# A fused two-block network on one core: expert weights asked for in smaller parts, slot-weight transposes inside the up product, and the last pair's gather in two parts

## What is computed

```python
x = x + g1 * (concatenate([y_l, fourier_mixer(f_l, w_four)]) @ w_out)
# hier_moe on t = modulate(rmsnorm(x, norm2), sh2, sc2), 256 tokens
grp = top_k(softmax(t @ w_rg + b_rg), 1)          # 1 of 4 groups
j_top = top_k(softmax(logits of that group), 2)   # 2 of its 8 experts
gate = p_top_grp * p_top / sum(p_top)
y[token] += gate * ((silu(xb @ w_eg[e]) * (xb @ w_eu[e])) @ w_ed[e])
out = rmsnorm(x + g2 * y, final_norm)
```

## Time and profile before

| | us |
|---|---|
| median of three runs | 1468.61 |
| lowest and highest | 1464.35, 1469.03 |
| profiled execution | 1465.74 |
| its span in the trace | 1463.9 |
| PE, DVE, ACT busy | 1322.8, 799.7, 611.3 |
| mean rate of the transfers | 262 GB/s |

### The profile page before, as it was taken

One profiled execution on the slowest core, in us unless ns is written; L12 is line 12 of the kernel. 1 busy time (PEld: TensorE's weight loads), 2 busy tenths in 40 slices (PEclk: granted clock), 3 DMA queues, 4 the chain that ended last, 5 costly groups with the idle time before them and its releaser, 6 DMA issues.

```text
span 1463.9 us, 26277 instructions
## 1 busy us (share of the span) xinstructions
PE 1322.8 (90%) x11196; PEld 1126.5 (77%) x11196; DVE 799.7 (55%) x1223; ACT 611.3 (42%) x946; POOL 85.5 (6%) x65
## 2 busy tenths in 40 slices
PE   7999999999999999999999999888977777777877
PEld 7989798999989888999989999678544344434535
DVE  5557847766467577876558896964112112111213
ACT  5553345444456666455446654753211111111112
POOL 2000000000003100221001000410000000000000
PEclk9999999999999999999999999998999999999998
DMA  9655347544574567355453050329999999999995
GB/s 374 228 204 192 116 173 295 193 174 173 192 312 167 206 275 282 136 200 189 173 211 144 32 231 1 159 101 424 423 427 427 427 427 427 427 428 427 427 427 228
DMA packets 29489, 383.47 MB, mean 262 GB/s; under 512 B 3344, under 2 KB 3488, under 8 KB 6208
## 3 DMA queue, kind: packets, MB, share of 16 engines
q1 hardware_dynamic: 28656, 377.71, 64.2%
q0 software_dynamic: 720, 4.10, 0.7%
HBM read 380.75 MB, written 1.05 MB: 261 GB/s over the span
## 4 chain that ended last, share of the span: by engine, by line
PE 57%; DMA 24%; DVE 11%; ACT 6%; issue 2%; SPq 0%; POOL 0%; DVEq 0%; ACTq 0%; POOLq 0%
PE ps L649 56%; DMA ring<-in_experts 24%; DVE w_lo L1880 3%; DVE work L1892 2%; ACT work L1356 1%; ACT w_hi L1356 1%; DVE work L1880 1%; ACT HM L1356 1%; DVE HM L1880 1%; ACT L1356 1%; DVE act L1880 1%; DMA ring<-in_dense 0%; ACT act L1356 0%; DVE work L2151 0%; DVE small L2048 0%
## 5 line engine op out<-in xcount | busy, mean ns | idle before, releaser
L1880 DVE TENSOR_TENSOR w_lo<-ring,w_hi 128x1024 fp32r<-128x1024 f32 x272 | 339.7, 1258 | 213.0 <-ACT w_hi L1356 212.6
L649 PE MATMUL ps<-in_hi,w_hi 128*128 128x256 f32 x1376 | 390.6, 284 | 17.6 <-DVE w_lo L1880 17.2
L649 PE MATMUL ps<-in_hi,w_lo 128*128 128x256 f32 x1376 | 387.1, 281 | 0.0
L649 PE MATMUL ps<-in_lo,w_hi 128*128 128x256 f32 x1376 | 386.8, 281 | 0.0
L1356 ACT ACTIVATE w_hi<-ring 128x1024 fp32r<-128x1024 f32 x272 | 286.1, 1056 | 236.0 <-PE ps L649 230.7
L649 PE MATMUL ps<-ring,work 128*32 128x256 f32 (+3 forms) x2528 | 204.8, 459 | 95.3 <-DMA ring<-in_experts 86.5
L649 PEld LDWEIGHTS ps<-in_hi,w_hi 128*128 128x128 f32 x1376 | 261.4, 190 | 22.7 <-issue 19.3
L649 PEld LDWEIGHTS ps<-in_lo,w_hi 128*128 128x128 f32 x1376 | 261.4, 190 | 0.3
L649 PEld LDWEIGHTS ps<-in_hi,w_lo 128*128 128x128 f32 x1376 | 261.3, 190 | 0.0
L649 PEld LDWEIGHTS ps<-ring,work 128*32 128x32 f32 (+1 forms) x2528 | 85.4, 119 | 196.3 <-issue 112.3
L1892 DVE SCALAR_TENSOR_TENSOR X<-ps,mod,X 128x256 f32<-128x256 f32 x136 | 59.0, 479 | 248.3 <-PE ps L649 248.3
(11 more groups left out here) (270 smaller groups left out, 1894.7 us busy)
## 6 DMA issues: line engine op xcount, KB each, us to landing
ring<-in_experts SPq DMA_DIRECT2D x90, 2048.0 KB, 23.3
ring<-in_dense SPq DMA_DIRECT2D x82, 2048.0 KB, 8.0
ring<-in_dense SPq DMA_DIRECT2D x4, 512.0 KB, 8.3
work<-in_experts SPq DMA_DIRECT2D x1, 2048.0 KB, 11.5
ring<-in_experts SPq DMA_DIRECT2D x4, 512.0 KB, 21.5
spare<-in_experts SPq DMA_DIRECT2D x1, 1536.0 KB, 11.2
cst<-in_ret_cst POOLq DMA_DIRECT2D x1, 1280.0 KB, 13.1
cst<-in_experts SPq DMA_DIRECT2D x1, 1280.0 KB, 5.9
```

The source lines that it names most:

```text
L649: i = pe.matmul(o, l, r, start=start, stop=stop)
L1880: i = dve.tensor_tensor(out=o, in0=x, in1=y, op=op)
```

## The change

Three edits. First, SP asks for the held units in smaller parts. `cst`, `act2`, `work` 0 to 1024 and the first row of held unit 3 (`work` 1024 to 1536) wait only until PE is done with the last tile `y`; held unit 2 waits for the last `y_ready`; `lr2` still waits for `h_ready`, now behind the load of slot 5; the other four rows of unit 3's first part still wait for `y_lo_ready`. So that `cst` is free, the squares of tiles 4 and 5 (`ysq[2]`) go to `lr2`. Second, PE transposes the slot weights within the up product, behind the gather, and DVE reduces them and writes `SGt` before it makes `hs`. Third, in the last pair only four of the gather's eight pieces are made within the up product and the other four behind the transposes of `hs`, and ACT scales all eight behind its copy of `hT`. The pieces now lie at the same columns of the bank whichever is the first (`c * PAIR`), and the first part of the last gather signals nothing.

```diff
-        ysq = [at(9728, 512), at(10240, 512), at(2048, 512, of=flat_cst), at(0, 512, of=flat_sq)]
+        ysq = [at(9728, 512), at(10240, 512), lr2[:, :, :].rearrange("p a b -> p (a b)"), at(0, 512, of=flat_sq)]
...
             hold(1, spare[:, :], 0)
             first_load(0)
-            sp.wait_ge(s["h_ready"], KD)
+            await_full(sp, TILE["y", KX - 1])
             hold(0, flat_cst, 0)
             hold(0, act2[:, :, :].rearrange("p a b -> p (a b)"), 5)
-            hold(0, lr2[:, :, :].rearrange("p a b -> p (a b)"), 7)
+            hold(1, work[:, 0:2 * FE], 6)
+            hold(3, work[:, 2 * FE:3 * FE], 0)
+            sp.wait_ge(s["y_ready"], KX)
             hold(2, work[:, 9728:9728 + UNIT], 0)
             sp.wait_ge(s["chunk_used"], MIX0 + 2)
             first_load(5)
+            sp.wait_ge(s["h_ready"], KD)
+            hold(0, lr2[:, :, :].rearrange("p a b -> p (a b)"), 7)
             sp.wait_ge(s["y_lo_ready"], KX)
-            hold(1, work[:, 0:2 * FE], 6)
-            hold(3, work[:, 2 * FE:7 * FE], 0)
+            hold(3, work[:, 3 * FE:7 * FE], 1)
             sp.wait_ge(s["chunk_used"], MIX0 + FG)
...
-            HELD_PARTS = 3, 2, 1, 2, 2
+            HELD_PARTS = 3, 2, 1, 3, 2
...
-                    o = ps[:, bk, (c - first) * PAIR:(c - first + 1) * PAIR]
+                    o = ps[:, bk, c * PAIR:(c + 1) * PAIR]
                     for tau in range(2):
                         i = mm(o, t_raw[:, tau, c * P:(c + 1) * P], S2[:, tau, :], tau == 0, tau == 1)
-                i.then_inc(s["gath_full"], 1)
+                if first + count == KD or bk != GATHER_BANK:
+                    i.then_inc(s["gath_full"], 1)
...
                             if up and c == 4:
                                 pe.wait_ge(s["eq_ready"], pair + 2)
-                                gather(0, GATHER_BANK)
+                                gather(0, GATHER_BANK, KD // 2 if last else KD)
+                                pe.wait_ge(s["sgb_ready"], pair + 1)
+                                for tau in range(2):
+                                    i = pe.transpose(ps[:, Y_BANK, tau * P:(tau + 1) * P], SGb[:, tau, :], ident[:, :])
+                                i.then_inc(s["sg_full"], 1)
...
-                    pe.wait_ge(s["sgb_ready"], pair + 1)
-                    for tau in range(2):
-                        i = pe.transpose(ps[:, Y_BANK, tau * P:(tau + 1) * P], SGb[:, tau, :], ident[:, :])
-                    i.then_inc(s["sg_full"], 1)
                     pe.wait_ge(s["hs_ready"], pair + 1)
                     for b in range(2):
                         i = pe.transpose(ps[:, 0, b * P:(b + 1) * P], hs[:, b * P:(b + 1) * P], ident[:, :])
                     i.then_inc(s["ht_full"], 1)
+                    if last:
+                        gather(KD // 2, GATHER_BANK, KD // 2)
                     pe.wait_ge(s["ht_ready"], pair + 1)
...
-                    gathered(1 - p % 2, 0, GATHER_BANK, KD, pair + 3)
+                    if not last:
+                        gathered(1 - p % 2, 0, GATHER_BANK, KD, pair + 3)
                     act.wait_ge(s["ht_full"], pair + 1)
                     fn(hT[:, :, :].rearrange("p a b -> p (a b)"), ps[:, 0, 0:T], ACT.Copy, s["ht_ready"])
                     if last:
+                        gathered(1 - p % 2, 0, GATHER_BANK, KD, pair + 3)
                         load_norm_tables()
...
                     select(p + 1)
-                    dve.wait_ge(s["gs_ready"], pair + 1)
-                    dve.wait_ge(s["gu_full"], pair * 2 + 2)
-                    tt(hs, gs, ps[:, 1, 0:T], MUL, s["hs_ready"])
                     dve.wait_ge(s["sg_full"], pair + 1)
                     weighted = ps[:, Y_BANK, 0:T]
                     dve.tensor_reduce(gcol, weighted, AX_X, ADD).then_inc(s["gcol_ready"], 1)
                     ts(SGt[0:PAIR, 0, :], weighted[0:PAIR], 0.0, ALU.is_gt)
                     ts(SGt[PAIR:P, 1, :], weighted[PAIR:P], 0.0, ALU.is_gt, inc=s["sgt_ready"])
+                    dve.wait_ge(s["gs_ready"], pair + 1)
+                    dve.wait_ge(s["gu_full"], pair * 2 + 2)
+                    tt(hs, gs, ps[:, 1, 0:T], MUL, s["hs_ready"])
```

More of the change, by code:

```diff
@@ L1838, in gathered @@
                 for c in range(first, first + count):
-                    fn(xg[:, par, c, :], ps[:, bk, (c - first) * PAIR:(c - first + 1) * PAIR], ACT.Identity, s["xg_ready"],
+                    fn(xg[:, par, c, :], ps[:, bk, c * PAIR:(c + 1) * PAIR], ACT.Identity, s["xg_ready"],
                        scale=coef[:, 2, c:c + 1], bias=mod[:, 3 * KD + c, 0:1])
```

## The result

| | before | changed |
|---|---|---|
| median of nine executions each | 1466.71 us | 1470.67 us |
| lowest and highest | 1464.35, 1471.61 | 1466.5, 1473.55 |
| ratio, with its 95% interval | 1 | 1.0024 (1.0013 to 1.0034) |

The changed kernel is slower by 0.24%, 3.5 us, with an interval of 1.9 to 5.0 us. The forecast was 0.45 us. The profiled execution of the changed kernel has a span of 1468.6 us.

The account below looks back on a forecast made before the run. Expert-weight transfers were taken to bound the kernel from about 978 us, PE's chain its end. Terms -1.5 + 1.95 = +0.45 us, on a mean of 1466.9, gave 1467.4 us; range 1463 to 1471, 8 in 10 for 1461 to 1472.

Parts of the forecast that it names:

- What bounds the kernel: Whole kernel: expert-weight transfers bound everything from about 978 us; after the last landing at 1429.28 the chain is PE's.
- Part 1: Held units asked for 16.3 us earlier; only the backlog at 1023.97 is won: gain 9.1 - 7.6 = 1.5 us.
- The lower bound of 0.7: Earlier requests: least gain, 0.7 us, if what the engines lost around 1026 stays lost.
- Part 2: Slot weights transposed within the up product: gain 0.1 us for each pair, vanishing in PE's waits for units in 15.
- Part 3: Last pair's gather in two parts: ACT's scaling delays the last down product, cost 1.95 us.
- rival C: Tail: PE's clock falls behind the waits before the last down product; up to +10 us, 1472 to 1477; 9%.
- Rival A: Held units: the earlier start counts in full, -16.3 + 1.95, so 1451 us; 5%.
- Rival B: Start of pair 0: if PE's clock comes back early, it starts 6 us sooner, giving 1461 us; 11%.
- Rivals D: Transfers beside the last heads and `mix_out` (962 to 978) slow engines there: +5 us, 1472; 4%.
- E: Last pair: ACT's scaling doesn't hold PE up, -1.5 - 0.1, 1465.3 us; 12%.
- The sum: Whole kernel: -1.5 + 1.95 = +0.45 us on the profiled execution, 1465.74 to 1466.2 us.
- The level of 1467.4: Forecast time of the changed kernel, taking the mean of four times before, 1466.9 us, as the level.

Follow-up runs that it names:

- part 1 alone: Kernel before with only the earlier requests for held units: ratio 1.0003 (0.9993 to 1.0013).
- the late requests: Kernel before with its held requests waiting for six chunks of `mix_out`, the first going out 4.6 us behind `h_ready`: ratio 1.0024, 3.5 us slower.
- the 9 matmuls alone: Kernel before with 9 more matmuls into an unused bank while PE waits for the routing's mask: ratio 0.9994 (0.9985 to 1.0003).
- the split alone: Kernel before with only the last pair's gather in two parts: ratio 1.0029 (1.0016 to 1.0041), 4.3 us slower.
- the wait filled: Changed kernel with 12 more matmuls while PE would wait for ACT's scaling: ratio to before 1.0018 (1.0008 to 1.0028).
- the requests and the 9 matmuls: Kernel before with the earlier held requests and 9 more matmuls in PE's wait for the routing; slot 0 back 4.7 us sooner: ratio 0.9962, 5.6 us faster.

## Why the prediction failed, step by step

- **What bounds the kernel** held: the transfers to 1429, PE behind it. That the kernel before sits near the point where the two requests meet was in the working (a backlog of 1.5 us at 1023.97) and came out in the runs with 4.6 us later and 4.7 us earlier.
- **Part 1**: request times (961.4 forecast, 961.88), both dry stretches and the unmoved request at 1024 were right. The term was not: 1.5 us of backlog to be won, 0 measured (1.0003, and a landing 9.4 us after the request for 7.6). The landing out of an idle queue was taken as 7.6 us from two other places of the trace; at this place it took 9.4, and 9.2 with part 1 alone, as long as with the backlog before (9.1). The lower bound of 0.7 was still too high. The backlog was hardly one: before, the first reused slot was asked for 3.3 us ahead of the last held part's landing (1027.25) and landed 5.8 us behind it. Asked for 8.6 and 8.3 us ahead, with the late requests and with the 9 matmuls alone, it landed 4.9 us behind it. So 0.9 us was lost in that hand-over before, too. Of the kernels with part 1, the best starts the last gate half 404.7 us after that request, before 405.3: 0.6 us is the most that any of them won, and the changed kernel won nothing (405.6).
- **Part 2**: forecast 0.1 us and nothing elsewhere; the trace has 0.17, and 0.9996 (0.9986 to 1.0006) agrees.
- **Part 3**: PE's later start was forecast at 1.95 us and measured at 1.70 (14.88 against 13.18). What failed is that the sum put the matmuls behind the wait at their old time, with only ACT and the landings looked at for slack: the 2.57 us in which PE waits cost another 2.4 us, because the 96 records that follow run at the lower clock. That is rival C, to which I gave 9%, for spells of some 5 us or more, long enough to leave the bounds of no change. The working had counted 15 slow blocks among 22 behind waits of 2 us or more, and had priced one at 1.65 us, but put that price at nothing in the sum. It came in all three profiled kernels with this wait, ended with the block, and cost 2.41. So it was a term of the sum and not a rival: 1.70 + 2.41 = 4.1 us, and the split alone measured 4.3.
- **Rival A** (the start counts in full) fell with the requests alone. **Rival B** (slot 0 comes back sooner) didn't happen in the changed kernel, but its mechanism was right. Brought about with the 9 matmuls, slot 0 came back 4.7 us sooner, where the working had 6, and the kernel was 5.6 us faster than before. **Rivals D** and **E** fell: 1.0003 with part 1 alone, and ACT's scaling did hold PE up.
- **The sum**: -1.5 + 1.95 = 0.45 should have been 0 + 1.7 + 2.4 = 4.1; measured are 3.5 (1.9 to 5.0). The two misses, 1.5 us of gain that wasn't there and 2.4 us of clock that was left out, point the same way; only the wait, 0.25 too long, made up for a little. The level of 1467.4 was 0.7 above the median of before as measured now, the bound of 0.3% was not passed, and 1470.67 lies in the range; the forecast of next to no change did not hold.

## What to carry to other kernels

Before moving work behind the last stage's wait, follow its consumer: here four of eight pieces moved by 3 us took with them the scaling of all eight, which had been hidden and then stood in the chain. A new wait of PE ahead of a row of matmuls may have to be priced twice, the wait and the slower matmuls behind it (here 2.4 us behind 2.57 of wait, and nothing behind 2.25). And where two bounds lie within a us or two of each other, removing one shows nothing: test the second together with it before dropping the first.

## What the runs showed of the hardware

The same transfer of 2048 KB out of an idle queue doesn't always take the same time. Unit 4, asked for between 1002.2 and 1005.7, landed 7.6 to 8.7 us later in the seven kernels with part 1 (7.9 in the changed kernel, 7.6 with part 1 alone). The first reused slot took 9.4 and 9.2 in these two and 8.8 with the wait filled, but 7.9 to 8.3 in the four kernels that had part 1 and the 9 matmuls, though its neighbour was asked for 1.7 us behind it in all of them. The windows of the changed kernel (columns as above) show how such a transfer starts; a packet is counted in the window in which it starts:

```profile
1025.50:1026.00 0.50, 0.50 (x17) 0.27 (x12) 0.00 (x0) 0.38 (x1) 0.00 (x0) 1.00 1.41 262
1026.00:1026.50 0.50, 0.50 (x16) 0.31 (x12) 0.00 (x0) 0.00 (x0) 0.00 (x0) 1.00 0.00 0
1026.50:1027.00 0.50, 0.50 (x16) 0.15 (x8) 0.00 (x0) 0.00 (x0) 0.00 (x0) 1.00 0.77 328
```

The empty window isn't idle. From 1024.4 to 1026.4 the DMA view has 16 packets for 73.4% of 16 engines' time, 1.47 us a packet; from 1027.4 to 1029.4 it has 52 for 102.6%, 0.63 us a packet. So the first packets out of an idle queue were more than twice as slow. The first 2 us in the kernel with the requests and the 9 matmuls look alike (16 packets, 72.0%), and it landed its slot in 8.0 us; what makes 9.4 of 8.0 is open.

PE's granted clock fell within a single wait of 2.57 us, which was for ACT and not for data (1.00 until 1446.5, 0.50 from 1447), and came back with the end of the block. The block behind that wait was slow in three kernels of three, that behind 2.25 us was not (2.84 us), and that behind 1.91 and 2.26 us close together was (4.49). The Trainium skill (TensorE: Matmul & The Clock Gate, HAM oscillation) has the PE fall to its lower clock in waits for data between bursts. The rows bear it out in part.

The spread between executions may have a source of the same kind, before the stage that was changed. From 940 to 950 us PE's clock was 0.94 in the profiled execution of before and 0.79 in that of the kernel before with the 9 matmuls, which come only 60 us later; its first held request went out at 980.83, 3.1 us after that of the earlier trace rows. The clock there isn't the whole of it: with the wait filled it was 1.00, and the first held request went out at 962.86, 1.0 us later than in the changed kernel, where the clock was 0.92.
